# A four-stage transformer kernel: decays, sums, turning and the last additions in another order

## The reference

```python
g = -jnp.exp(a_log) * jax.nn.softplus(ba + dt_bias)      # delta rule: decays
gc = jnp.cumsum(g, axis=-1)                              # its running sums
dA = (dt * a)...; acs = jnp.cumsum(dA, axis=-1)          # scan: decays and their sums
out = out + combine[:, e:e + 1] * swiglu(xt, w_gate[e], w_up[e], w_down[e])
x = layer_norm(DEEPNORM_ALPHA * x + ffn, ln_g[i, 1], ln_b[i, 1])
```

## Time and profile before

| | us |
|---|---|
| median of 3 runs | 1676.19 (1676.14 to 1676.23) |
| profiled execution, its own time | 1676.79 |
| its span, first to last record | 1675.0 |
| TensorE matmuls busy | 1607.5 (96%) |
| VectorE / ScalarE busy | 1299.7 (78%) / 969.6 (58%) |

### The profile page before, as it was taken

How to read it: one execution, slowest core, us unless ns; L and a number is a source line. 1 busy time by engine, 2 the same in 40 slices (tenths; PEclk the granted TensorE clock), 3 DMA queues, 4 the chain that set the end, 5 groups by cost and what they waited for, 6 DMA issues and landing times.

```text
span 1675.0 us, 22668 instructions
## 1 busy us (share of the span) xinstructions
PE 1607.5 (96%) x8856; PEld 1364.0 (81%) x8856; DVE 1299.7 (78%) x1092; ACT 969.6 (58%) x827; POOL 40.4 (2%) x35
## 2 busy tenths in 40 slices
PE   6989999999989999999999999999999999999995
PEld 5878599998989777888888888888888888888883
DVE  3767554547657787988988988988988998988985
ACT  4323244443444553776777776777767777777771
POOL 3000000002000010000000000000000000000000
PEclk8999999999999999999999999999999999999998
DMA  9150165554544007999999999999999999999990
GB/s 323 36 201 1 51 226 183 193 177 150 161 142 151 27 26 252 361 389 342 357 372 345 370 352 341 369 356 349 370 348 344 369 359 343 363 354 358 362 332 27
DMA packets 210751, 441.04 MB, mean 263 GB/s; under 512 B 7172, under 2 KB 57568, under 8 KB 210656
## 3 DMA queue, kind: packets, MB, share of 16 engines
q1 hardware_dynamic: 208656, 434.42, 72.6%
q10 hardware_dynamic: 1440, 4.78, 0.8%
q0 software_dynamic: 560, 0.48, 0.2%
HBM read 438.61 MB, written 1.05 MB: 262 GB/s over the span
## 4 chain that ended last, share of the span: by engine, by line
PE 87%; DVE 8%; ACT 2%; issue 1%; POOL 1%; DMA 1%; POOLq 0%; DVEq 0%; ACTq 0%
PE ps L2146 18%; PE ps L2148 18%; PE ps L2147 18%; PE ps L1669 5%; PE ps L1671 5%; PE ps L1670 5%; PE ps L2141 2%; PE ps L1662 2%; PE ps L2171 1%; PE ps L1926 1%; PE ps L1927 1%; DVE w_lo L1040 1%; PE ps L1928 1%; DVE arena L1069 1%; ACT w_hi L658 1%
## 5 line engine op out<-in xcount | busy, mean ns | idle before, releaser
L1473 DVE TENSOR_TENSOR w_lo<-raw,w_hi 128x2048 fp32r<-128x2048 f32 x252 | 576.8, 2290 | 81.5 <-ACT w_hi L895 77.4
L895 ACT CAST w_hi<-raw 128x2048 fp32r<-128x2048 f32 x252 | 482.7, 1915 | 153.3 <-PE ps L2148 153.0
L1040 DVE TENSOR_TENSOR w_lo<-raw,w_hi 128x2048 fp32r<-128x2048 f32 (+1 forms) x73 | 169.0, 2321 | 132.5 <-ACT w_hi L658 132.5
L2146 PE MATMUL ps<-w_hi,xg_hi 128*128 128x512 f32 x672 | 268.1, 399 | 2.5 <-issue 1.7
L2148 PE MATMUL ps<-w_hi,xg_lo 128*128 128x512 f32 x672 | 262.5, 391 | 0.0
L2147 PE MATMUL ps<-w_lo,xg_hi 128*128 128x512 f32 x672 | 261.6, 389 | 0.0
L658 ACT CAST w_hi<-raw 128x2048 fp32r<-128x2048 f32 (+1 forms) x73 | 137.0, 1879 | 161.9 <-PE ps L1671 106.1
L1669 PE MATMUL ps<-xT_hi,w_hi 128*128 128x256 f32 x768 | 220.4, 287 | 0.3 <-DVE xT_lo L1033 0.3
L1670 PE MATMUL ps<-xT_lo,w_hi 128*128 128x256 f32 x768 | 219.6, 286 | 0.0
L1671 PE MATMUL ps<-xT_hi,w_lo 128*128 128x256 f32 x768 | 219.6, 286 | 0.0
L1473 DVE TENSOR_TENSOR xT_lo<-raw,xT_hi 128x2048 fp32r<-128x2048 f32 x84 | 192.3, 2289 | 31.2 <-ACT xT_hi L895 31.2
(11 more groups left out here) (373 smaller groups left out, 2251.4 us busy)
## 6 DMA issues: line engine op xcount, KB each, us to landing
raw<-in_moe_w_gate SPq DMA_DIRECT2D x112, 1024.0 KB, 6.4
raw<-in_moe_w_up SPq DMA_DIRECT2D x112, 1024.0 KB, 6.7
raw<-in_moe_w_down SPq DMA_DIRECT2D x112, 1024.0 KB, 6.3
raw<-in_ssm_w_in SPq DMA_DIRECT2D x20, 1024.0 KB, 5.4
raw<-in_ffn_w_gate SPq DMA_DIRECT2D x11, 1024.0 KB, 5.6
raw<-in_ffn_w_up SPq DMA_DIRECT2D x11, 1024.0 KB, 5.5
raw<-in_ffn_w_down SPq DMA_DIRECT2D x11, 1024.0 KB, 4.9
raw<-in_even_w_in SPq DMA_DIRECT2D x10, 1024.0 KB, 13.7
```

Source lines behind the costliest of these rows:

```text
L895: act.copy(e_hi((n + 2 * odd) % CUT_E), raw[:, i, :]).then_inc(sem("hi_made"), 1)
L1040: TTO(w_lo[:, c, 0:size], raw[:, i, 0:size], w_hi[:, c, 0:size].bitcast(F32), ALU.subtract).then_inc(d_lo_made, 1)
L1473: TTO(e_lo(c), raw[:, n % RAW, :], e_hi(c).bitcast(F32), ALU.subtract).then_inc(lo_made, 1)
L2146: mm(out_ap, hi, whi, start=start, stop=False)
```

## The change

- **Start.** Both tiles of x come on SP's queue, with a semaphore for each. TensorE runs 7 matmuls on zeros before the turning and 6 behind it. Piece 0 is rounded and subtracted in two halves, between the two tiles of x; the gate's matmuls wait for each part apart. The small transfers wait for piece 0, the parameter transposes stand behind the gate, and the copy to `pcol` behind piece 3's subtraction.
- **Delta rule's sums** stand between the two query pieces, and ScalarE rounds piece 11 ahead of the four logarithms.
- **Scan.** `dA` is made ahead of m = 6 instead of m = 7.
- **End.** The last expert's last piece finishes bank 5 before bank 6; the four quarters have four banks; the branch stands ahead of the last subtractions and additions, and these are interleaved with the layer norm; the last tile is scaled and stored in two halves.
- Some semaphores are shared (`z_made`, `bank7_made`, `router_made`).

```diff
 NPRE = N2 + N_OUT
-DT_AT, SP_AT, ACS_AT = 3, 5, 8
+DT_AT, SP_AT, DA_AT, ACS_AT = 3, 5, 6, 8
...
 PLACE_GATHER = START + 33
+LAST_BANKS, LONE_BANKS = (7, 4, 2, 3), (7, 4, 7, 4)
...
             sp.dma_start(x_tok[:, 0, :], dram["x"][0, 0:P, :]).then_inc(sem("x_loaded"), 16)
+            sp.dma_start(x_tok[:, 1, :], dram["x"][0, P:2 * P, :]).then_inc(sem("x1_loaded"), 16)
...
-            pool.wait_ge(sem("x_loaded"), 48)
+            pool.wait_ge(raw_loaded[0], 16)
...
             act.dma_start(const[:, 0:P], dram["shape_consts"][:, 0:P]).then_inc(sem("x_loaded"), 16)
-            act.dma_start(x_tok[:, 1, :], dram["x"][0, P:2 * P, :]).then_inc(sem("x_loaded"), 16)
...
-            turn_high(0)
-            for n in range(CUT):
+            turn_high(0, (0, 1))
+            act.wait_ge(raw_loaded[0], 16)
+            act.wait_ge(d_piece_used, 1)
+            act.copy(w_hi[:, 0, 0:PIECE // 2], raw[:, 0, 0:PIECE // 2]).then_inc(sem("first_high"), 1)
+            act.copy(w_hi[:, 0, PIECE // 2:PIECE], raw[:, 0, PIECE // 2:PIECE]).then_inc(sem("dense_hi_made"), 1)
+            turn_high(0, (2, 3))
+            for n in range(1, CUT):
                 dense_high(n, n, n, 1)
...
             act.activation(e2dn[:, :, :], adn[:, :, :], ACT.Ln, bias=1.0).then_inc(sem("dn_e2"), 1)
+            n = N0 - 1
+            dense_high(n, n % RAW_D, n % CUT, n // RAW_D + 1)
             for b in range(4):
...
                 act.activation(rn[:, 512 * b:512 * b + 512], ps[:, b, :], ACT.Ln, bias=eps_rms[:, 0:1]).then_inc(sem("norm_ln"), 1)
-            n = N0 - 1
-            dense_high(n, n % RAW_D, n % CUT, n // RAW_D + 1)
             for b in range(4):
...
                 for h in range(2):
+                    if by_half:
+                        act.wait_ge(*((sem("first_half_done"), 1), (piece_used, count(PPE, it, (CUT_E + n + 1))))[h])
                     act.copy(oe_hi[:, h, :], ps[:, 5 + h, :]).then_inc(sem("oe_hi_made"), 1)
...
-            for t in range(TT):
-                act.wait_ge(sem("ln_done"), TT * 3 + t + 1)
-                act.dma_start(out[0, t * P:(t + 1) * P, :], yacc[:, t, :]).then_inc(sem("out_stored"), 16)
-            act.wait_ge(sem("out_stored"), 16 * TT)
+            act.wait_ge(sem("ln_done"), TT * 3 + 1)
+            act.dma_start(out[0, 0:P, :], yacc[:, 0, :]).then_inc(sem("out_stored"), 16)
+            for b in range(2):
+                act.wait_ge(sem("ln_done"), TT * 3 + 2 + b)
+                cs = slice(512 * b, 512 * b + 512)
+                act.dma_start(out[0, P:2 * P, cs], yacc[:, 1, cs]).then_inc(sem("out_stored"), 16)
+            act.wait_ge(sem("out_stored"), 16 * 3)
...
-            turn_low(0)
-            for n in range(CUT):
+            turn_low(0, (0, 1))
+            for ready, cs in ((sem("first_high"), slice(0, PIECE // 2)), (sem("dense_hi_made"), slice(PIECE // 2, PIECE))):
+                dve.wait_ge(ready, 1)
+                last = TTO(w_lo[:, 0, cs], raw[:, 0, cs], w_hi[:, 0, cs].bitcast(F32), ALU.subtract)
+                last.then_inc(sem("first_low") if cs.start == 0 else d_lo_made, 1)
+            turn_low(0, (2, 3))
+            for n in range(1, CUT):
                 dense_low(n, n, n)
-            dve.wait_ge(sem("params_turned"), 1)
-            dve.wait_ge(sem("taps_loaded"), 16 * 11)
-            dve.tensor_copy(pcol[:, 0:CONV * NXBC], ps[:, 7, 0:CONV * NXBC])
-            dve.tensor_copy(pcol[:, P:P + 88], ps[:, 7, P:P + 88]).then_inc(sem("params_copied"), 1)
-            dve.wait_ge(sem("params_copied"), 1)
...
                 dense_low(n, n % RAW_D, n % CUT)
+                if m == 0:
+                    dve.wait_ge(sem("bank7_made"), 1)
+                    dve.wait_ge(sem("taps_loaded"), 16 * 11)
+                    dve.tensor_copy(pcol[:, 0:CONV * NXBC], ps[:, 7, 0:CONV * NXBC])
+                    dve.tensor_copy(pcol[:, P:P + 88], ps[:, 7, P:P + 88]).then_inc(sem("params_copied"), 1)
+                    dve.wait_ge(sem("params_copied"), 1)
                 if m in N_DN:
...
-                if m == ACS_AT - 1:
+                if m == DA_AT:
                     dve.wait_ge(sem("ssm_sp"), 2)
...
-            expert_rest((0, E - 1), 1, None, E - 1, None, rank)
+            expert_rest((0, E - 1), 1, None, E - 1, None, rank, False)
             more = dve.value_load(over[0:1, 0:1].bitcast(I32), min_val=0, max_val=SEQ)
-            dve.wait_ge(sem("e_added"), 4 * E + FIRST)
             with dve.If(more > 0):
+                output_end(E - 1, (0, E - 1), LAST_BANKS)
+                dve.wait_ge(sem("e_added"), 4 * E + FIRST)
                 with dve.Fori(0, E - 1, 2) as i:
...
-            layer_norm(3, [(sem("e_added"), 4 * E + FIRST)] * TT, x=yacc, add=False)
...
+            last_it = (0, E - 1)
+            def statistics(t):
+                for b in range(2):
+                    dve.wait_ge(sem("last_added"), 2 * t + b + 1)
+                    last = dve.bn_stats(stats[:, t, b, :], yacc[:, t, 512 * b:512 * b + 512])
+                link(last)
+                link(dve.bn_aggr(mv[:, t, :], stats[:, t, :, :].rearrange("p b s -> p (b s)")))
+                TS(mv[:, t, 1:2], mv[:, t, 1:2], LN_EPS, None, ALU.add).then_inc(sem("ln_var"), 1)
+            def centre(t):
+                link(STT(yacc[:, t, :], yacc[:, t, :], mv[:, t, 0:1], ln_gb[:, 0, :], ALU.subtract, ALU.mult))
+            def scale(t, cs):
+                dve.wait_ge(sem("ln_rstd"), TT * 3 + t + 1)
+                STT(yacc[:, t, cs], yacc[:, t, cs], rstd[:, t:t + 1], ln_gb[:, 1, cs], ALU.mult, ALU.add).then_inc(sem("ln_done"), 1)
+            for h in range(2):
+                output_low(last_it, h)
+            for q in range(2):
+                add(E - 1, last_it, q, LAST_BANKS[q], sem("last_added"))
+            statistics(0)
+            for q in range(2, 4):
+                add(E - 1, last_it, q, LAST_BANKS[q], sem("last_added"))
+            dve.wait_ge(sem("ln_loaded"), 32 * 4 + 16)
+            centre(0)
+            statistics(1)
+            scale(0, slice(0, D))
+            centre(1)
+            for b in range(2):
+                scale(1, slice(512 * b, 512 * b + 512))
...
-            def halves(n, width, place):
+            def halves(n, width, place, between=None):
                 for half in range(2):
+                    if half and between:
+                        between()
                     c = (n + half) % CUT
-                    pe.wait_ge(d_lo_made, RAW_D + n + half + 1)
+                    if n + half:
+                        pe.wait_ge(d_lo_made, RAW_D + n + half + 1)
                     whi, wlo = [w[:, c, 0:4 * width].rearrange("p (k n) -> p k n", k=4) for w in (w_hi, w_lo)]
...
                         ts_ = slice(t * P, (t + 1) * P)
+                        if n + half == 0:
+                            pe.wait_ge(sem("xT_lo_made"), 2 * t + 2)
                         for kk in range(4):
                             k = 4 * half + kk
+                            if n + half == 0 and t == 0 and kk == 0:
+                                pe.wait_ge(sem("first_low"), 1)
+                            if n + half == 0 and t == 0 and kk == 2:
+                                pe.wait_ge(d_lo_made, RAW_D + 1)
                             mm(place(t), xT_hi[:, k, ts_], whi[:, kk, :], start=k == 0, stop=False)
...
-            pe.wait_ge(sem("x_loaded"), 48)
-            turn(0)
+            def warm_up(n):
+                for _ in range(n):
+                    mm(ps[:, 7, :], zerob[:, 0:P], zerob[:, :], start=True, stop=True)
             pe.sem_inc(d_piece_used, CUT)
+            pe.wait_ge(sem("pool_set"), 2)
+            warm_up(7)
+            pe.wait_ge(sem("x_loaded"), 32)
+            turn_tile(0, 0)
+            pe.wait_ge(sem("x1_loaded"), 16)
+            turn_tile(0, 1)
+            warm_up(6)
+            halves(N_GATE, 512, lambda t: ps[:, 4 + t, :])
             pe.wait_ge(sem("taps_loaded"), 16 * 11)
             pe.transpose(ps[:, 7, 0:CONV * NXBC], prow_a[0:CONV * NXBC, :], ident[0:CONV * NXBC, 0:CONV * NXBC])
-            pe.transpose(ps[:, 7, P:P + 88], prow_b[0:88, :], ident[0:88, 0:88]).then_inc(sem("params_turned"), 1)
-            pe.wait_ge(sem("xT_lo_made"), 4)
-            halves(N_GATE, 512, lambda t: ps[:, 4 + t, :])
+            pe.transpose(ps[:, 7, P:P + 88], prow_b[0:88, :], ident[0:88, 0:88]).then_inc(sem("bank7_made"), 1)
...
+            def running_sums():
+                pe.wait_ge(sem("dn_gb"), 1)
+                pe.wait_ge(sem("norm_ln"), 4)
+                pe.wait_ge(sem("ln_loaded"), 16 * 3)
+                g8 = gdn[:, :, :].rearrange("p t h -> p (t h)")
+                mm(ps[:, 3, 0:8], tri, g8, start=True, stop=True)
+                mm(ps[:, 3, 8:12], ones[:, :], gdn[:, 0, :], start=True, stop=True).then_inc(sem("dn_gc"), 1)
             pe.wait_ge(sem("dn_conv"), NDN // 2)
-            halves(N_Q, 512, lambda t: ps[:, 6 + t, :])
```

(59 more changed lines are left out.)

49 lines of the change are left out of this document (22 added, 27 removed).

## The result

The changed kernel took 1653.91 us, the median of four runs (1651.68 to 1656.43), against 1676.21 before: a ratio of 0.9864, with a 95% interval of 0.9852 to 0.9875. 1652.3 had been forecast, with a range of 1648.0 to 1657.5. The profiled execution after is the fastest, 1651.68, so between the two profiled executions 25.1 us are gone, between the medians 22.3. The two figures differ because the four runs after lie 4.75 us apart.

The account below looks back on a forecast made before the run. TensorE, dense at full clock elsewhere, was taken to lose time at four waiting places; 9.6 + 6.4 + 1.0 + 6.9 = 23.9 us off 1676.79, less 0.6, gave 1652.3 us, range 1648.0 to 1657.5.

Parts of the forecast that it names:

- A, the start: Start: gate waits for x turned and piece 0's first half, until 11.0; columns begin at 22.3, not 31.94; 9.6 us gained.
- rival (1): Start: the clock is low when the gate starts, costing 2.4 us, so 1654.7; chance 0.13.
- B, the sums: Delta rule: half the 48 matmuls go ahead of the sums, which wait 0.9 us; 6.4 us gained, bounds 4 and 7.
- C, the scan: Scan: TensorE's 8.0 us wait ahead of m=8 becomes 6.6 ahead of m=9; 1.0 us gained, bounds 0 and 2.
- rival (4): Scan: the wait of 8.0 us and the low clock after it go wholly; 8.8 more gained, 1643.5; chance 0.02.
- the bank's reader: Scan: m=9 uses the sums' bank and waits until VectorE has read them, at 475.3; 6.6 us of waiting.
- D, the end: End: vector part ends 6.3 us sooner, half-size last store saves some 0.6; 6.9 us gained, bounds 5 and 7.5.
- The branch's cover: End: the branch is taken while VectorE waits for TensorE, 1646.9 to 1652; without that cover it costs 3.1 us again.
- The gate's matmuls at low clock: Start: a sign of being wrong: the gate's matmuls start after 12 or take 0.43 us each.
- the sum of 23.9: Whole kernel: gains of 9.6, 6.4, 1.0 and 6.9 us at start, delta rule's sums, scan and end.

Follow-up runs that it names:

- again: The kernel after itself, unchanged, run once more on another chip: 1651.57 us (1649.61 to 1652.10).
- u_end: The kernel after with all edits of the end taken back to the kernel before: 1658.14 us (1657.14 to 1661.38).
- late_branch: The kernel after with VectorE's branch for tokens over the limit put behind the last four additions: 1656.47 us (1653.60 to 1657.62).
- u_scan: The kernel after with the scan's decays made one piece later, as in the kernel before: 1652.22 us (1649.54 to 1654.88).
- w_none: The kernel after with no warm-up matmuls on zeros at all: 1652.71 us (1652.21 to 1657.27).
- logs_first: The kernel after with ScalarE's four logarithms ahead of rounding the last query piece, as before; TensorE's order as after: 1656.67 us (1653.51 to 1657.40).
- cols6: The kernel after with VectorE's reading of the scan's sums moved ahead of the convolution of m=6: 1644.48 us (1643.88 to 1649.60).
- u_sums: The kernel after with the delta rule's sums ahead of both query halves and the last piece rounded behind the logarithms, as before: 1658.76 us (1657.55 to 1660.49).
- w16: The kernel after with 16 matmuls on zeros instead of 6 behind the turning of x: 1651.87 us (1650.97 to 1652.91).

## Why the prediction was right, and where it was not

**A, the start, 9.6 forecast, 7.8 measured.** The order of events was right: piece 0's first half sets the gate (11.35 for 11.0, since piece 0 was there 0.2 later than forecast and the two steps on it took 0.15 more), the small transfers are not waited for, no weight is late. The term that was off is the clock: rival (1) came to pass in this execution and took 1.7, less than its 2.4. I gave it 0.13; of the nine profiles with this very start four have the fall (after, again, u_end, late_branch), and their columns begin at 23.8 to 24.05. In the other five they begin at 22.3 to 22.7, where 22.3 was forecast, so the start is then 9.3 to 9.65 better than before. From u_scan, where they begin at 22.29, the window that corresponds to 12 to 16 above, and the row:

```profile
12.00:16.00 4.00, 4.00 (x19) 3.32 (x18) 3.66 (x4) 2.90 (x2) 3.73 (x7) 1.00 1.10 334
...
22.29 0.36 PE L1723 MATMUL ps<-xT_hi,w_hi 128*128 128x256 f32 x1
```

The Trainium skill's page "TensorE: Matmul & The Clock Gate", Part 1, says that the low clock is the default and activity releases it; w_none's slow transposes (3.65 instead of 2.21) agree.

**B, the sums, 6.4 forecast, 6.3 measured,** between VectorE's 7.8 and 14.1. The sums waited 1.0 (0.9 forecast), the clock stayed, VectorE's column values ended at 85.66, 0.3 before TensorE's halves, as forecast. logs_first shows why both orders had to change together.

**C, the scan, 1.0 forecast, 0.8 from before to after and 1.65 from after to u_scan in the traces, no difference in the medians.** The wait of 6.76 ahead of m=9, ended by the column read, is the forecast one (6.6). cols6 proves the reason: with the reader alone moved, it goes. What the sum had no room for is that the reader could be moved as well; rival (4), 8.8 more, did not come to pass with this change, as the bank's reader spoke against it; 6.3 to 7.1 more come once that reader is early.

**D, the end, 6.9 forecast, 7.1 measured,** u_end the same 7.1. The branch's cover is worth 2.5 to 3.1 of it by late_branch and u_end; the rest is the earlier bank 5, the vector work ordered by tile and half the last bytes, which no run tells apart.

**What I said would make me wrong.** The gate's matmuls at low clock were one of my signs and did come, and cost what is said above. From 492 us of before to the end of the experts nothing moved by 0.3. What I didn't name is the stretch between the delta rule and the scan: 3.1 of the profiled difference are two falls at 428 to 438 that the profiled execution of before has and that of after has not. I don't count them as a gain of the change: nothing in the diff touches that place, and u_sums, w16, w_none and late_branch, which carry most or all of the change, have one or two of them too. With a single profile of before it isn't shown how often that kernel has them. The four parts measured add up to 22.0. Between the medians, the sum of 23.9 stands against 22.3 on the first chip and, with the kernel after run again, 24.3 on another. It was right, and by chance more exact than a single execution of either kernel is.

What stays open: I have one profile for each kernel, two for the kernel after, so how often a place falls is counted over kernels that differ elsewhere, and whether w16 holds the gate's clock in every execution isn't shown.

## What to carry to other kernels

When a consumer is moved earlier, follow the bank or buffer that it uses to its last reader and move that too: the scan's decays one piece ahead were worth about 1 us in the traces, the reader of their sums another 6 to 7. A wait and the low clock after it are one price, and a block of narrow matmuls can bring the low clock too (1.7 us here). Compare two profiled executions place by place, and take no difference for the change's that stands where nothing was changed.

## What the runs showed of the hardware that I had not expected

TensorE's granted clock falls to its lower level, 1.2 GHz, with the engine busy all the time, as the profile counts it: behind a block of 16 matmuls of 8 columns (3.6 us long) 1.7 us were lost in ten profiles of twelve and 3.4 in the two others, and behind 16 of 32 columns 1.7 or 3.4 in five of twelve. With the matmuls of 8 columns dealt out between wide ones the clock stayed whole, in both profiles that do so. The Trainium skill's page "TensorE: Matmul & The Clock Gate", Part 1, names idling as what brings the low clock; in the windows with a fall behind such a block (6.00 of 6.00 us busy from 38 to 44) the profile shows no idling.

The same kernel doesn't take the same time twice. Nine runs of the kernel after lie between 1649.6 and 1656.4, nine of the kernel before on one chip between 1674.4 and 1678.1. In some pairs of runs half of the difference is in the mean clock, in others none.

A fall need not cost anything: the one at 100 to 106 in the kernel after, while the delta rule's chain ran over VectorE and ScalarE, left the distance of the two traces at 14.1 on both sides.
